# RWKV scores of a hybrid diffusion step: one key buffer for both heads of a pair, and 64-row score products

## The reference

```python
def rwkv7_scan(r, decay, k, v, a, b, s0, reverse):
    '''S_t = S_{t-1} diag(decay_t) + (S_{t-1} a_t) b_t^T + v_t k_t^T ; y_t = S_t r_t.'''
    def step(S, inp):
        r_t, d_t, k_t, v_t, a_t, b_t = inp
        sa = jnp.einsum('bhvk,bhk->bhv', S, a_t)
        S = S * d_t[:, :, None, :] + sa[..., None] * b_t[:, :, None, :] + v_t[..., None] * k_t[:, :, None, :]
        return S, jnp.einsum('bhvk,bhk->bhv', S, r_t)
...
    kk = kk / jnp.maximum(jnp.linalg.norm(kk, axis=-1, keepdims=True), 1e-12)
    k_dir = k[:, :, None, :] * (1.0 + (a - 1.0) * k_a)
    for d in range(2):
        y_d, s_d = rwkv7_scan(rh, heads(decay[:, :, d]), k_d, vh, -kk, kk * a_d, s0[:, d], d == 1)
    y = ys[0] + ys[1]
```

## Time and profile before

| | |
|---|---|
| median of 3 runs | 2317.68 us |
| span of the profiled execution, first to last instruction | 2312.3 us |
| median of the runs less this span | 5.4 us |
| PE busy | 2050.3 us (89%) |
| PE weight loads busy | 1435.5 us (62%) |
| DVE busy | 614.1 us (27%) |
| ACT busy | 326.0 us (14%) |
| POOL busy | 41.1 us (2%) |
| mean granted PE clock | 0.943 |
| RWKV stage | 191 to 505 us |

### The profile page before, as it was taken

The page is one execution under the profiler, slowest core; times in us unless marked ns, Lnnn a source line. Parts: engine busy times, 40 slices in busy tenths (PEclk is TensorE's granted clock), DMA queues, the critical chain, the costliest instruction groups (busy, mean ns, idle before and its releaser), DMA issues. The chain is left out here.

```text
span 2312.3 us, 27555 instructions
## 1 busy us (share of the span) xinstructions
PE 2050.3 (89%) x11534; PEld 1435.5 (62%) x11535; DVE 614.1 (27%) x1261; ACT 326.0 (14%) x610; POOL 41.1 (2%) x65
## 2 busy tenths in 40 slices
PE   5997897789999898788888979997979998998997
PEld 3876887687888687777766534454534454444443
DVE  4436566542000354566622000001000001000002
ACT  1012222210000133222211100010000010000001
POOL 0001000000000000000000000000000000000000
PEclk8998998899999999889897999999999999999998
DMA  8739211102443341300014997789997789876760
GB/s 325 286 123 426 108 74 74 74 9 109 149 159 129 155 146 37 151 10 10 10 46 197 428 358 286 291 361 425 427 407 291 287 323 426 334 285 255 285 223 19
DMA packets 37093, 492.38 MB, mean 213 GB/s; under 512 B 4380, under 2 KB 4541, under 8 KB 7325
## 3 DMA queue, kind: packets, MB, share of 16 engines
q1 hardware_dynamic: 36956, 490.33, 54.0%
HBM read 487.95 MB, written 2.36 MB: 212 GB/s over the span
## 5 line engine op out<-in xcount | busy, mean ns | idle before, releaser
L2009 PE MATMUL bank<-ring,arena 128*128 128x512 f32 x896 | 399.7, 601 | 39.5 <-issue 39.5
L2009 PEld LDWEIGHTS bank<-ring,arena 128*128 128x128 f32 x896 | 169.9, 193 | 240.3 <-issue 240.3
L2083 DVE TENSOR_TENSOR arena<-bank,arena 128x256 f32<-128x256 f32 (+1 forms) x56 | 31.3, 559 | 866.3 <-PE bank L2009 565.0
L2005 PE MATMUL bank<-ring,arena 128*64 128x256 f32 x1792 | 210.5, 391 | 22.8 <-issue 22.6
L2025 PE MATMUL bank<-ring,arena 128*128 128x512 f32 x448 | 197.3, 593 | 2.7 <-ACT arena L1981 2.7
L2005 PEld LDWEIGHTS bank<-ring,arena 128*64 128x64 f32 x1792 | 129.5, 140 | 94.9 <-issue 39.2
L1231 PE MATMUL bank<-arena,ring 128*128 128x256 f32 x704 | 155.3, 383 | 4.0 <-DVE arena L292 3.8
L2025 PEld LDWEIGHTS bank<-ring,arena 128*128 128x128 f32 x448 | 84.9, 190 | 108.8 <-issue 105.1
L1231 PEld LDWEIGHTS bank<-arena,ring 128*128 128x128 f32 x704 | 134.1, 192 | 24.4 <-issue 4.1
L1352 PE MATMUL bank<-arena,ring 128*128 128x256 f32 x512 | 115.6, 388 | 6.4 <-DVE arena L292 3.8
L701 PE MATMUL bank<-arena 128*128 128x128 f32 x768 | 102.5, 289 | 14.0 <-issue 9.9
(11 more groups left out here) (346 smaller groups left out, 1982.6 us busy)
## 6 DMA issues: line engine op xcount, KB each, us to landing
ring<-in_experts SPq DMA_DIRECT2D x168, 2048.0 KB, 10.1
ring<-in_stream SPq DMA_DIRECT2D x61, 2048.0 KB, 11.8
arena<-in_masks SPq DMA_DIRECT2D x1, 1280.0 KB, 5.8
xT<-in_xT SPq DMA_DIRECT2D x1, 1024.0 KB, 6.8
arena<-in_s0gd SPq DMA_DIRECT2D x4, 256.0 KB, 3.3
out_sgd<-arena SPq DMA_DIRECT2D x4, 256.0 KB, 2.5
out_y<-arena SPq DMA_DIRECT2D x4, 256.0 KB, 2.5
arena<-in_hfw SPq DMA_DIRECT2D x1, 544.0 KB
```

What stands on the lines that cost most here:

```text
L2005: mm = nc.tensor.matmul(out[HALF * c:HALF * c + HALF, 0:256], hA[:, j, 0:HALF], w[:, j, 256 * c:256 * c + 256], start=(j == 0), stop=(j == ...
L2009: mm = nc.tensor.matmul(out[:], hA[:, j, :], w[:, j, :], start=(j == 0), stop=(j == DC - 1))
L2083: V.tensor_tensor(actb[:, k % 2, 0:n], ps[2 * (k % 2) + 1][:, 0:n], sgl[:, k % 2, 0:n], ALU.mult)\
```

## The change

The key buffer `bk` exists once. Both heads' keys are written in one go over all 128 partitions, and the buffer has no zero rows. Each score product takes only the 64 partitions of its head, as a row tile of PE's array (`tile_position` 0 or 64), and the two heads follow each other within every kind of product. The token-major keys come from two real transposes instead of four products with the identity.

```diff
-        bk = [take(2, TT) for _ in range(2)]
+        bk = take(2, TT)
...
-                for part in (*bk, s0s[0], AT[0], Ab[0], s0s[1], AT[1], Ab[1]):
+                for part in (s0s[0], AT[0], Ab[0], s0s[1], AT[1], Ab[1]):
...
-                        for q in range(4):
-                            s, hh = divmod(q, 2)
+                        for s in range(NS):
                             tok = slice(s * T, (s + 1) * T)
                             for i in range(2):
-                                nc.tensor.matmul(ps[q][:, i * TT:(i + 1) * TT].rearrange("p (a t) -> p a t", a=2),
-                                                 bk[hh][:, i, tok], ar[g][:, :, tok], start=True, stop=True)
-                            mm = nc.tensor.matmul(ps[4 + hh][:, s * T:(s + 1) * T], ar[g][:, 0, tok], bk[hh][:, 0, tok],
-                                                  start=True, stop=True)
+                                for hh in range(2):
+                                    rows = slice(64 * hh, 64 * hh + 64)
+                                    nc.tensor.matmul(ps[2 * s + hh][:, i * TT:(i + 1) * TT].rearrange("p (a t) -> p a t", a=2),
+                                                     bk[rows, i, tok], ar[g][rows, :, tok], start=True, stop=True,
+                                                     tile_position=(64 * hh, 0))
+                            for hh in range(2):
+                                rows = slice(64 * hh, 64 * hh + 64)
+                                mm = nc.tensor.matmul(ps[4 + hh][:, s * T:(s + 1) * T], ar[g][rows, 0, tok], bk[rows, 0, tok],
+                                                      start=True, stop=True, tile_position=(64 * hh, 0))
...
                         for i in range(2):
-                            for hh in range(2):
-                                mm = nc.tensor.matmul(ps[6][:, TT + i * T:TT + (i + 1) * T], bk[hh][:, i, 0:T], ident,
-                                                      start=(hh == 0), stop=(hh == 1))
+                            mm = nc.tensor.transpose(ps[6][:, TT + i * T:TT + (i + 1) * T], bk[:, i, 0:T], ident)
...
-                            dve.wait_ge(s_zero, 3)
+                            dve.wait_ge(s_zero, 1)
...
-                            dve.wait_ge(s_zero, 6)
+                            dve.wait_ge(s_zero, 4)
...
-                        for i, f in enumerate((avs[g], kd)):
-                            for hh in range(2):
-                                rows = slice(64 * hh, 64 * hh + 64)
-                                ins = V.tensor_tensor(bk[hh][rows, i, :], sgs[g][rows], f[rows], ALU.mult)
-                                if (i, hh) != (1, 1):
-                                    dve_link.last(dve, ins)
-                        ins.then_inc(s_unit, 1)
+                        dve_link.last(dve, V.tensor_tensor(bk[:, 0, :], sgs[g], avs[g], ALU.mult))
+                        V.tensor_tensor(bk[:, 1, :], sgs[g], kd, ALU.mult).then_inc(s_unit, 1)
...
-                            dve.wait_ge(s_zero, 5 + 3 * g)
+                            dve.wait_ge(s_zero, 3 + 3 * g)
```

## The result

| | before | changed |
|---|---|---|
| median of 4 runs | 2317.76 us (2315.84 to 2318.26) | 2294.18 us (2292.63 to 2297.37) |
| ratio | | 0.9903, 95% interval 0.9889 to 0.9917 |
| span of the profiled execution | 2312.3 us | 2291.9 us |
| PE busy | 2050.3 us | 2029.8 us |
| DVE busy | 614.1 us | 607.1 us |

The account below looks back on a forecast made before the run. PE and DVE waiting for each other in turn around eight score bursts was taken as the bound. 8.0 + 16.6 - 0.7 - 2 = 21.9 us; 2312.3 - 21.9 + 5.4 = 2295.8 us, range 2289.5 to 2305.

Parts of the forecast that it names:

- Key products: Ahead of each score burst, two 128-partition products instead of four make each round 1.0 us shorter, 8.0 us in all.
- Score products: In the eight score bursts, two row tiles overlap fully, 2.17 us instead of 4.34 at full clock; 16.6 us gained.
- no DVE wait in the first burst: Sign for the first burst (c=0, g=0): DVE no longer waits there, 1.06 us of wait gone.
- 2.7 us instead of 4.87 in c=0, g=0: Sign for the score overlap, written for c=0, g=1: burst 2.7 us instead of 4.87 to where DVE goes on.
- Change of shape: PE's return from 64-row tiles costs 0.1 us in each of seven bursts, 0.7 us lost.
- Transposes: Behind the bursts, two key transposes replace four identity products; PE saves 0.65 us per burst, hidden, so nothing gained.
- The clock in the inversions: Four inversions: longer PE idle time ahead lowers the clock, 2 us lost; bounds 8.9 us gained to 5 lost.
- The later stages shift as a whole: Behind the RWKV stage: the full DMA ring moves on only when PE frees slots, so the gain is kept.
- A: Rival, chance 0.10: tiles overlap but weight loads don't hide, 0.1 us per pair; gain 13.3 us, 2304.4 us.
- B: Rival, chance 0.05: no overlap, tiles run one after another, 4.34 us a burst as before; 2310.4 us.
- C: Rival, chance 0.03: each row-tile change waits for an empty array, 0.16 us, 12 times a burst; slower, 2335 us.
- D: Rival, chance 0.10: overlap, but low clock costs inversions 5 us and five bursts' tails 1 us each; 2304 us.

Follow-up runs that it names:

- e1: Changed kernel with the keys again written by four vector products on 64 partitions into the one buffer; 2299.51 us, 0.9922 of before.
- e4: Changed kernel with the two key transposes replaced by four products with the identity; 2292.18 us, 0.9887 of before.
- e6: Changed kernel with unused filler products on PE ahead of the five slow bursts and each inversion, three PE waits moved up; 2282.20 us, 0.9843 of before.
- e8: Kernel before the change, with filler products at the same places (three instead of five ahead of each inversion); 2300.96 us, 0.9921 of before.
- e2: Changed kernel with score products contracted over all 128 partitions, no row tiles, so scores sum both heads; 2303.23 us, 0.9944 of before.
- e5: Changed kernel with score products grouped by head, three of one then three of the other per sequence; 2299.30 us, 0.9904 of before.
- e7: e6 with ACT's copy of the adaLN sums for g=0 moved ahead of the exponentials of g=1; 2282.16 us, 0.9844 of before.
- e9: Changed kernel with filler products ahead of the bursts alone, none ahead of the inversions; 2286.59 us, 0.9853 of before.
- e10: Changed kernel with filler products ahead of the inversions alone, none ahead of the bursts; 2287.21 us, 0.9864 of before.
- e3: Kernel before with only the score products changed to alternating 64-row tiles, each from its own key buffer; 2298.72 us, 0.9919 of before.

## Why the prediction was right, point by point

**Key products, 8.0 us.** Right: 7.9 us by e1, and the products stand as forecast, 0.34 us apart. The sign that I gave for it, PE's waits in g=1 shorter by 1.0 us each, is missed: they are some 0.5 shorter, because I had not seen that PE, with its transposes, also comes to them sooner.

**Score products, 16.6 us, with 0.7 us back for the change of shape.** Right in the sum. Together 15.9 us forecast; the bursts are 50.5 - 34.8 = 15.7 us shorter. Full overlap was the step that carried it, and it holds: 2.17 us from first to last pass against 4.34. By bursts it was less even. In c=0, g=0 I gave 1.06 us; 0.68 came, since L359 now waits for ACT, whose copy stands behind the exponentials of g=1; my sign "no DVE wait in the first burst" is missed, there is one of 0.51 us. In c=0, g=1 I gave 2.17 and 1.1 came, because of the stop of PE before L933; in c=1, g=1, without it, 2.0. (My sign "2.7 us instead of 4.87 in c=0, g=0" contradicts my own sum, which leaves 4.94 - 1.06 = 3.9 there; 4.87 is the burst of g=1.) The slow bursts gave 2.0, 1.3, 3.1, 2.5 and 3.0 us where 1.6, 1.6, 2.2, 2.9 and 2.9 were forecast. The assumption that they run at the low clock nearly throughout held for three of the five (0.50) and in part for two (0.62, 0.63). Where it held, I had still priced what stands behind the last score in g=0 at its 0.6 us of full clock; it took 1.15, so those two bursts are 5.37 us and not 5.0.

**Change of shape, 0.1 us a burst.** Right: in c=0, g=1 the last score pass starts at 220.30 and L359 at 220.50, 0.20 apart instead of 0.11. But g=0's L359 doesn't see it.

**Transposes, nothing.** Right by e4 as far as the stage can tell: 0.7 us the other way.

**The clock in the inversions, 2 us lost.** Wrong in its sign in this profile: the inversions took 1.2 us less. The price was wrong too: I had put the clock's cost in the inversions before at 8.9 us, half of the time at the low level, but with all four at 1.00 (e6, e8) they take 132.4 us against 137.1, 4.7 us less. What covers the rest no run tested. Over the kernels without fillers their sum lies between 134.5 and 137.5 us, so neither a loss nor a gain can be told. The row on which the worry rested, the longer idle time before L701, is there (3.19 us against 2.53), and two inversions behind it kept 1.00.

**The later stages shift as a whole.** Right: 1801.8 us behind the stage against 1801.1.

**The sum.** 21.9 us forecast, 24.9 in the stage and 22.5 by the ratio; 2295.8 us forecast, 2294.18 measured. Of the 3 us that the stage gave more, the inversions are the whole: 1.2 gained for 2 lost. That part was luck, since their clock varies by more than this between kernels, and so it is in part for the sum of the bursts, met to 0.2 us: the first two bursts gave 1.4 us less than I had written for them, the five slow ones 0.6 us more. The 5.4 us that I added for launch and end are 1.7 of that and 3.7 of a short profiled execution; the sum starts from the median either way, so nothing else hangs on it.

**The rivals.** A (weight loads in the open, 0.1 us a pair) is out: eight loads in 0.74 us beside eight matmuls, pairs 0.22 us apart. So the rule that I had cited from the Trainium skill, "TensorE: Matmul & The Clock Gate", Part 3, that a weight load overlaps running matmuls only when the row group differs, does not describe these passes: the second pass of a head loads its weights while the first runs on the same rows (in the burst above a load from 209.41 to 209.60 us, beside a pass that starts at 209.41 and whose follower starts at 209.63). B and C are out by the same rows, and e2 shows what B would have looked like. D is out: the inversions did not lose, though the longer ends of the two g=0 bursts at 0.50 are what it described.

## What to carry to other kernels

Two fp32 products that each contract over 64 rows run in the time of one as row tiles 0 and 64 with outputs in different banks, weight loads included; let the tiles alternate product by product, since grouping them gave back a quarter of the gain in a burst. (Outputs in one bank were not tried.) A row of short PE bursts between waits for another engine pays twice: once for its length and once for the clock that falls in the wait, and a few products without use in the idle time can be worth a good part of the algorithmic change (here 9.7 us of stage on top of 24.9). When a piece gets shorter, look at what stands in front of its successor on the third engine (here ACT's exponentials before a copy), because that was late next here.

## What the runs showed of the hardware that I had not expected

**PE starts passes ahead of the order of the code.** In e5 a pass on row tile 64 started 0.54 us behind the burst's first, while three passes on tile 0 that stand before it in the code had not started. How far ahead it can look no run tested.

**A stop of PE in the second burst.** In the changed kernel, in e4 to e7 and in e9 and e10 PE stops once in the burst c=0, g=1: the distance between two passes there is 1.01, 0.74, 0.78, 0.87, 1.28, 0.54 and 1.20 us instead of 0.22 or less. It stops after the second pass in e4 and after the eighth in the others. In each of these seven traces a 16 KB packet of the instruction queue starts 2.39 to 2.54 us before PE goes on (216.48 and 218.99 us in the changed kernel, 214.87 and 217.37 in e4, 214.00 and 216.42 in e5, 214.55 and 217.05 in e6, 215.45 and 217.99 in e7, 214.31 and 216.70 in e9, 214.17 and 216.60 in e10). In the kernel before, e1, e3 and e8, whose slower key products hold PE back a microsecond longer, and in e2, whose passes are half as fast, no such distance is seen: by the same 2.5 us their instructions would have been there in time. It fits an engine that has run out of loaded instructions behind the 256 short ones of L347; no run tested that alone, so it stays an inference from twelve traces. The stop itself costs 0.3 to 1.1 us once in the kernel.

**How much of the time is the clock.** With 4.2 us of idle time ahead, bursts of the changed kernel ran at 0.50 to 0.63; with the fillers in the same place, all at 1.00. Ahead of the inversions the idle time right in front doesn't decide alone: in the changed kernel 3.19 us were followed by 1.00 twice, and 2.97 and 2.72 us by 0.91 and 0.93, while 3.20 us in e1 (c=1) were followed by 0.91. With the fillers, which leave 0.6 to 1.2 us of idle time there, all four were at 1.00 (e6, e7, e8, e10).
